# Eight experts of a mixture layer: three passes over split operands on the whole array, or plain float32 on four column strips

## What is computed

```python
logits = xf @ router_w
top_logits, top_idx = lax.top_k(logits, 2)
gates = softmax(top_logits)
# for each expert e, over the tokens that chose it:
y = (silu(xb @ w_gate[e]) * (xb @ w_up[e])) @ w_down[e]      # 1024 -> 3584 -> 1024
out[token] += gate * y
```

## Time and profile before

| | us |
|---|---|
| median of 3 runs | 1414.14 (1412.26 to 1416.24) |
| the profiled execution | 1417.15 |
| its span, first to last instruction | 1415.4 |
| TensorE matmul busy | 1337.0 (94%) |
| TensorE weight load busy | 991.8 |
| DVE busy | 843.4 (60%) |
| ACT busy | 735.3 (52%) |
| granted TensorE clock, mean | 0.98 |
| moved by DMA | 417.39 MB, mean 295 GB/s |

### The profile page before, as it was taken

The page is one execution under the profiler, slowest core; times in us unless marked ns, Lnnn a source line. Parts: engine busy times, 40 slices in busy tenths (PEclk is TensorE's granted clock), DMA queues, the critical chain, the costliest instruction groups (busy, mean ns, idle before and its releaser), DMA issues.

```text
span 1415.4 us, 16234 instructions
## 1 busy us (share of the span) xinstructions
PE 1337.0 (94%) x6696; PEld 991.8 (70%) x6696; DVE 843.4 (60%) x902; ACT 735.3 (52%) x949; POOL 0.2 (0%) x4
## 2 busy tenths in 40 slices
PE   6998999999999799999799999979999999979996
PEld 6776999997786588853378863358888885337885
DVE  4666555555665688820188840078889882009884
ACT  5666444445665477720267730067777772017772
POOL 0000000000000000000000000000000000000000
PEclk9999999999999799999999999989999999999998
DMA  9903553474403089999999999999999999999970
GB/s 361 388 6 119 179 179 120 138 246 171 144 36 119 1 319 362 371 358 407 404 409 408 402 363 409 402 409 409 402 355 347 361 372 358 408 404 409 408 303 31
DMA packets 126688, 417.39 MB, mean 295 GB/s; under 512 B 3344, under 2 KB 8080, under 8 KB 126480
## 3 DMA queue, kind: packets, MB, share of 16 engines
q1 hardware_dynamic: 126608, 416.29, 76.9%
HBM read 415.23 MB, written 1.05 MB: 294 GB/s over the span
## 4 chain that ended last, share of the span: by engine, by line
PE 83%; DMA 6%; DVE 5%; ACT 3%; SPq 2%; issue 1%; DVEq 0%; ACTq 0%
PE ps L506 21%; PE ps L508 21%; PE ps L507 21%; PE ps L925 8%; DMA ring<-moe_g 5%; PE ps L916 2%; SPq L467 2%; PE ps L874 1%; PE ps L488 1%; DVE scratch L1489 1%; DVE ring_lo L1758 1%; DMA ring<-w_in 1%; PE ps L634 1%; ACT scratch L1091 1%; DVE xgT_lo L1764 1%
## 5 line engine op out<-in xcount | busy, mean ns | idle before, releaser
L1758 DVE TENSOR_TENSOR ring_lo<-ring,e_hi 128x2048 fp32r<-128x2048 f32 x210 | 479.3, 2290 | 131.9 <-ACT e_hi L1255 131.6
L1255 ACT ACTIVATE e_hi<-ring 128x2048 fp32r<-128x2048 f32 x210 | 402.4, 1921 | 181.8 <-PE ps L508 156.4
L506 PE MATMUL ps<-e_hi,xgT_hi 128*128 128x512 f32 x560 | 227.9, 407 | 27.9 <-DVE xgT_lo L1764 27.9
L508 PE MATMUL ps<-e_hi,xgT_lo 128*128 128x512 f32 x560 | 223.0, 398 | 0.0
L507 PE MATMUL ps<-ring_lo,xgT_hi 128*128 128x512 f32 x560 | 222.7, 398 | 0.0
L1597 DVE TENSOR_TENSOR d_lo<-ring,d_hi 128x1024 fp32r<-128x1024 f32 x82 | 100.4, 1224 | 95.1 <-ACT d_hi L1199 94.9
L925 PE MATMUL ps<-ring,xgT_s 128*64 128x512 f32 (+1 forms) x768 | 149.5, 542 | 5.2 <-DMA ring<-moe_u 5.2
L506 PEld LDWEIGHTS ps<-e_hi,xgT_hi 128*128 128x128 f32 x560 | 107.1, 191 | 59.0 <-DVE xgT_lo L1764 30.7
L1199 ACT ACTIVATE d_hi<-ring 128x1024 fp32r<-128x1024 f32 x82 | 86.9, 1059 | 112.8 <-PE ps L508 112.8
L508 PEld LDWEIGHTS ps<-e_hi,xgT_lo 128*128 128x128 f32 x560 | 106.9, 191 | 26.4
L507 PEld LDWEIGHTS ps<-ring_lo,xgT_hi 128*128 128x128 f32 x560 | 107.1, 191 | 23.9
(11 more groups left out here) (268 smaller groups left out, 1790.2 us busy)
## 6 DMA issues: line engine op xcount, KB each, us to landing
ring<-moe_g SPq DMA_DIRECT2D x56, 2048.0 KB, 12.9
ring<-moe_u SPq DMA_DIRECT2D x56, 2048.0 KB, 13.8
ring<-moe_d SPq DMA_DIRECT2D x56, 2048.0 KB, 12.5
ring<-w_in SPq DMA_DIRECT2D x6, 2048.0 KB, 11.4
ring<-dense_g SPq DMA_DIRECT2D x5, 2048.0 KB, 7.9
ring<-dense_u SPq DMA_DIRECT2D x5, 2048.0 KB, 7.9
ring<-dense_d SPq DMA_DIRECT2D x5, 2048.0 KB, 8.8
ring<-w_out SPq DMA_DIRECT2D x4, 2048.0 KB, 15.2
```

The source lines that it names most:

```text
L506: pe.matmul(out, hi_l, hi_r, start=start, stop=False, skip_group_check=True)
L508: return pe.matmul(out, lo_l, hi_r, start=False, stop=stop, skip_group_check=True)
L1255: nc.scalar.activation(hi_slot(g, s, q), slot_of(no)[:, r * E_PIECE:(r + 1) * E_PIECE], ACT.Copy).then_inc(act_done, act_p.step((g, s, "le ...
L1758: nc.vector.tensor_tensor(slot_lo(no)[:, part], slot_of(no)[:, part], hi_slot(g, s, q).bitcast(F32), ALU.subtract).then_inc(dve_done, dve_ ...
```

## The change

All eight experts now run as plain float32 with no high and low parts, on four 32-column strips of the array. Tokens are taken in rounds of 32: three rounds for a full expert (room for 96 tokens), two for a small one (64). In a round each of the four strips holds the same 32 tokens and takes a quarter of the weight columns: 256 of 1024, or 128 of the last 512. `e_hi`, `ring_lo`, `xgT_lo`, `hidT_lo`, `y_lo` and their ACT and DVE work are gone; TensorE waits for the unit's DMA alone. The gathered rows' evictions are shared, four chunks on ACT and four on DVE. The gate goes into the scatter matrix (`pick_g`, transposed to `pick_gT`), and the scatter uses four strips of 32 rows, each into a bank of its own. The tables of places are now those of the small expert for all, with one scatter after unit 0. The loop for overflow has two rounds over the experts of 96 tokens each. The last scatter stands behind the `If`, and the output leaves in four quarters, each once it is added, instead of two halves after all.

```diff
-E_PIECE, E_SPLIT = 2048, 4
+STRIP, STRIPS = 32, 4
+BIG, LITTLE = 3, 2
+CAPACITY = [BIG * STRIP] * N_FULL + [LITTLE * STRIP] * (NE - N_FULL)
+ROUNDS = 2
+SCATTER_AFTER = 0
+SCATTER_BANKS = (2, 3, 6, 7)
+HID_T_AFTER = {U_LAST["u", c] + 1: c for c in range(NGU)}
+PICK_T_AFTER = U_LAST["d", 1] + 1
+GATHER_AFTER = U_FIRST["d", NCH - 3]
...
-            sp.wait_ge(result_ready, 1)
-            for a in range(TT):
-                sp.dma_start(out[0, a * P:(a + 1) * P, :], xres[:, a, :]).then_inc(out_stored, 16)
+            for q in range(2 * TT):
+                a, part = q // 2, slice(q % 2 * CH, (q % 2 + 1) * CH)
+                sp.wait_ge(result_ready, q + 1)
+                sp.dma_start(out[0, a * P:(a + 1) * P, part], xres[:, a, part]).then_inc(out_stored, 16)
...
+                def unit(s, it, n):
...
+                    if kind == "d":
+                        for j in range(CH // P):
+                            if c < NCH - 1:
+                                quarter, part, parts = c % 2 * 2 + j // 2, j % 2, 2
+                            else:
+                                quarter, part, parts = j, 0, 1
+                            for t in range(nt):
+                                x0 = (t * parts + part) * P + quarter * STRIP
+                                for q in range(STRIPS):
+                                    ins = pe.matmul(ps[q * STRIP:(q + 1) * STRIP, 4 + t // 2, t % 2 * T:(t % 2 + 1) * T],
+                                                    hidT[:, c // 2 % 2, x0:x0 + STRIP],
+                                                    w[:, j * D + q * T:j * D + (q + 1) * T],
...
+                    else:
+                        cols = GU_COLS[c]
+                        wide, b0 = cols // STRIPS, 0 if kind == "g" else 2
+                        for i in range(UNIT // cols):
+                            k = h * (UNIT // cols) + i
+                            for t in range(nt):
+                                b, c0 = divmod(t * wide, CH)
+                                for q in range(STRIPS):
+                                    ins = pe.matmul(ps[q * STRIP:(q + 1) * STRIP, b0 + b, c0:c0 + wide],
+                                                    xgT[:, k, t * STRIP:(t + 1) * STRIP],
+                                                    w[:, i * cols + q * wide:i * cols + (q + 1) * wide],
...
+                def gates_T(s, it):
+                    pe.wait_ge(act_done, at((g, s, "hidT", 1), it))
+                    for t in range(strips(g, s)):
+                        for a in range(TT):
...
+            def scatter(nt):
+                for t in range(nt):
+                    for a in range(TT):
+                        for q, bank in enumerate(SCATTER_BANKS):
+                            rows_q = slice(q * STRIP, (q + 1) * STRIP)
+                            ins = pe.matmul(ps[:, bank, a * T:(a + 1) * T],
+                                            pick_gT[rows_q, (t * TT + a) * P:(t * TT + a + 1) * P],
+                                            y[rows_q, t * T:(t + 1) * T], ...)
...
-                        nc.scalar.activation(hi_slot(g, s, q), slot_of(no)[:, r * E_PIECE:(r + 1) * E_PIECE],
-                                             ACT.Copy).then_inc(act_done, act_p.step((g, s, "lead", q)))
...
-                        nc.vector.tensor_tensor(slot_lo(no)[:, part], slot_of(no)[:, part], hi_slot(g, s, q).bitcast(F32),
-                                                ALU.subtract).then_inc(dve_done, dve_p.step((g, s, "rest", q)))
```

More of the change, by code:

```diff
@@ L215, in at @@
         if it is None:
-            return start + (NE - 1) * k + m
+            return start + (self.known["trips", loop, name] - 1) * k + m
         assert start + m - back * k > 0
@@ L327, in trunk_program @@
         hT_flat = hT[:, :, :].rearrange("p k t -> p (k t)")
[L328 to L332, removed]
+        sig, hid = hT_flat[:, 0:768], hT_flat[:, 768:1536]
+        rows, y = xn[:, 0, :], xn[:, 1, 0:BIG * T]
+        ps_flat = ps[:, :, :].rearrange("p b n -> p (b n)")
         moved = hT_flat[:, 1024:1024 + 2 * TT * NE * NE].rearrange("p (a e) -> p a e", e=NE)
@@ L773, in gathered_T @@
                             ins.then_inc(pe_done, pe_p.step((g, s, "gathered", k // 4)))
-                def scatter(a, key):
-                    for n in range(2):
-                        part = slice(n * CH, (n + 1) * CH)
-                        pe.matmul(ps[:, 6 + n, :], pickT[:, a * P:(a + 1) * P], y_hi[:, part], start=True, stop=False)
-                        ins = pe.matmul(ps[:, 6 + n, :], pickT[:, a * P:(a + 1) * P], y_lo[:, part], start=False,
-                                        stop=True)
-                        ins.then_inc(pe_done, pe_p.step(key + ("scatter", 2 * a + n)))
@@ new lines, in expert @@
+                def expert(s, it=None):
+                    pe.wait_ge(act_done, at((g, s, "xgT_a")) if g == 0 else before(g, s, it, "xgT_a"))
+                    pe.wait_ge(dve_done, at((g, s, "xgT_d")) if g == 0 else before(g, s, it, "xgT_d"))
+                    for n in range(M_UNITS):
+                        unit(s, it, n)
+                        if n == SCATTER_AFTER and (g or s):
+                            pe.wait_ge(act_done, at((g, s, "y"), it))
+                            scatter(strips_before(g, s)).then_inc(pe_done, pe_p.step((g, s, "scatter")))
+                        if n in HID_T_AFTER:
+                            hidden_T(s, it, HID_T_AFTER[n])
+                        if n == PICK_T_AFTER:
+                            gates_T(s, it)
+                        if n == GATHER_AFTER and (g or s < NE - 1):
+                            pe.wait_ge(act_done, at((g, s, "hidT", 2), it))
@@ L1282, in small_expert @@
[L1282 to L1294 removed]
+                    nt = strips(g, s)
@@ new lines, in expert @@
+                def expert(s, it=None):
+                    if g or s:
+                        dve.wait_ge(pe_done, at((g, s, "scatter"), it))
+                        for q in range(4):
+                            a, n = q // 2, q % 2
+                            part = xres[:, a, n * CH:(n + 1) * CH].rearrange("p (b n) -> p b n", b=2)
+                            b = SCATTER_BANKS[2 * n]
+                            nc.vector.tensor_tensor(part, ps[:, b:b + 2, a * T:(a + 1) * T], part,
+                                                    ALU.add).then_inc(dve_done, dve_p.step((g, s, "add", q)))
+                    for c in range(NGU):
+                        w = strips(g, s) * GU_COLS[c] // STRIPS
+                        dve.wait_ge(act_done, at((g, s, "silu", c), it))
+                        dve.wait_ge(pe_done, at((g, s, "unit", U_LAST["u", c]), it))
+                        nc.vector.tensor_tensor(hid[:, 0:w], ps_flat[:, 2 * CH:2 * CH + w], sig[:, 0:w],
+                                                ALU.mult).then_inc(dve_done, dve_p.step((g, s, "hid", c)))
+                        if c == 2 and (g or s < NE - 1):
+                            dve.wait_ge(pe_done, at((g, s, "pick_g_T"), it))
+                            picks(s if g else s + 1, it + 1 if g else s + 1)
+                    if g or s < NE - 1:
+                        gathered_out(s if g else s + 1, it)
```

514 lines of the change are left out of this document (140 added, 374 removed).

## The result

The changed kernel takes 1391.02 us in the median (1390.13 to 1393.09, 4 runs) against 1413.60 for the kernel before, measured beside it; the ratio is 0.984, 95% interval 0.9821 to 0.9859. That is 22.6 us less where 52 were forecast (1362). The profiled execution took 1391.69 us with a span of 1389.9.

The account below looks back on a forecast made before the run. Full experts were taken as bound by TensorE, small ones by the DMA. Expert times summed to 857 us after 489.7, plus 5 for bookkeeping and 11.5 for the ending, adjusted by +1.8 and -3.0: 1362 us, range 1338 to 1470.

Parts of the forecast that it names:

- PE's blocks of instructions: Expert stage: one 16 KB block in 7 us, 2.4 GB/s of 406; costed at nothing, 6 us as the other end.
- The same 5.17 and 3.45: Two units of the last 512 columns: twice the records at half the length, 5.17 us full and 3.45 small.
- Rival B: Narrow units: a floor per record of 27 to 54 ns; at 54 they double, about 1407 us; chance 0.10.
- Four strips at once, 5.17 and 3.45 for wide units: Wide expert units: four strips run fully concurrently, a unit taking 5.17 us in a full expert, 3.45 in a small one.
- A: Every expert unit: strips cost 8% more than their columns, 1396 us; inside the forecast's range, together chance 0.62.
- C: All expert units: a floor above 54 ns per record makes TensorE's issue the bound, slower than before; chance 0.16.
- D: Expert units: only two strips work at once, units of 10.3 and 6.9 us, about 2096 us; chance 0.09.
- Visits and scatter: Full-array work between units: visits 7.2 us a full expert, 6.3 a small one, scatter 2.9; experts 118.7 and 81.6.
- Returns: Three changes from a small to a full expert: the 7.6 us wait goes, unit 0 starts when it lands.
- The lead: Ring ahead of TensorE: 23.5 us when full, at 5.17 us a unit; small experts take 83.5, 97 and 87 us.
- Start and ending: First unit starts about 487.7, plus 2 us for half speed; after the last unit 11.5 us instead of 14.1.
- E: Overflow loop: lowered capacities overflow, adding 16 more experts, +1900 us; chance 0.03 together with the unforeseen.

Follow-up runs that it names:

- e4: Changed kernel with each matmul of the narrow units split in two of 64 columns, twice the instructions; 1466.06 us (one run).
- e10: Changed kernel with every wide gate and up matmul split in two of 128 columns and each unit's transfer cut to its first quarter; 1377.79 us (one run).
- e1: Changed kernel with each expert unit's weight transfer cut to its first quarter, TensorE's program the same; 1337.86 us (one run).
- e2: Changed kernel with two token rounds of the narrow units on strip pairs with 256 columns, fewer instructions; 1373.29 us, 0.9708 of before.
- e6: Changed kernel with narrow units recut to fewer instructions and four small experts, visited first, fourth, seventh and last; 1360.67 us, 0.9623 of before.

## Why the prediction was wrong, step by step

**The step that failed: PE's blocks of instructions, "I cost it at nothing, with 6 us as the other end".** I had counted right, one block in 7 us, and then weighed the blocks by their bytes: 2.4 GB/s of 406. What counts is the time of a round against the time that TensorE needs for 256 instructions. Under the ring's full traffic the round is 6.2 us (the four blocks from 1132.30 on), with little traffic 3.75 (the idle stretch of e4, and the sum that fitted e10). A wide unit uses 192 instructions in 5.17, a block in 6.9 us: it just fits. A narrow one uses 384, a block in 3.45, and runs dry. Units 16 to 18 of the five full experts took 20.0, 22.3, 22.0, 24.2 and 21.5 us instead of 15.5, 32 us in all. The sum of the full experts shows it: 118.7 forecast, 122.1 to 127.8 measured, 125 to 128 before. Taking it away gave 17.7 (1391.0 to 1373.3); part came back as waiting for landings.

**"The same 5.17 and 3.45" for narrow units.** Rival B named these units and the sign that would show them (7 to 10 us), and gave them 0.10, but with a floor per record as its mechanism. That one falls: 28 ns a record inside the bursts of 128 columns and 14 ns with 64 (e4), and 5.2 us a narrow unit where the traffic is light (e1). The sign "wrong if any TensorE unit of a full expert exceeds 5.9 us" came true in unit 17 of all five and in 16 or 18 of three of them, and so did its reason, that full experts are then no faster than today. By its letter it also caught units with a visit, for which the forecast itself had 6.1 and more.

**Four strips at once, 5.17 and 3.45 for wide units: right.** 5.2 and 3.5 (3.4 with 512 columns), 96 records in 5.06 to 5.2 us. As the forecast said, four records start together (within 21 ns) and the next four 0.216 us after them; in the mean one starts every 53 to 54 ns. Rivals A, C and D fall. The 62 ns per MATMUL that the Trainium skill (TensorE: Matmul & The Clock Gate, "Wait — 56ns, not 53.3ns?") gives for hardware decoding off would put 5.95 us on a wide unit: this trace has 5.2, so it didn't apply here, and no run tells which decoding was on. The floor of about 25 ns between starts that the same section gives doesn't hold across strips either: e4 starts a record every 14 ns on the array, which is one in 56 ns on each strip.

**Visits and scatter: right.** 6.1 for a unit with six transposes (5.17 + 0.92), 7.6 with the gather, 6.3 with the eight transposes, 7.3 and 8.1 with a scatter (8.07 expected). A full expert at 118.4 and a small one at 81.9 in e1, against 118.7 and 81.6.

**ACT and DVE at nothing: right.** Behind the first unit one unit waits for them, 0.6 us (unit 0 of the eighth visit, for an ACT copy), and three quarters of their time is idle. **Returns: right.** Unit 0 of the three full experts behind a small one takes 5.3, 6.7 and 6.1; above 5.2 stand a wait for a landing in the second and mostly that ACT copy in the third.

**The lead: too good by the rate of the transfers.** With 5.17 us a unit I had small experts of 83.5, 97 and 87 us against 81.6 of work, with the returns about 25 us of dry time in all. With the holes gone it is 37 (6.5, 18.1, 9.6 and 2 x 1.5 in e2), and a unit needs 5.27 on the long run (e6). The same bookkeeping with 5.27 gives 102 and 94 for the fourth and the seventh visit, where e2 has 100.0 and 91.6: the rate explains the difference and a little more. By its own numbers the sum was also too kind to the second visit, which gives up 25.0 us of a lead of 23.5. This is the second error: from 1362 to the 1373 of e2 it is 11 us, and from there to 1391 it is the blocks.

**Start and ending.** The first unit began at 483.3 against 487.7. In the other kernels this point lies between 482.9 and 487.0, so these 4.4 us were in part luck, and they hid part of the miss: from the first unit's start to the last unit's end it is 31 us (864 forecast, 895 measured). At half clock the first unit cost 2.8 more where I had 2. The ending took 11.3 against 11.5, by two errors that cancel: 2.3 us before the last scatter in which TensorE waits for nothing shown (a block of instructions lands 1.5 us before their end, and e1 has 2.1 us there with a light DMA; that the branch for the overflow, which stands there, brings them was not tested), and a last store of 2.7 instead of 4.3. **E** didn't happen.

## What to carry to other kernels

When a change makes an engine's instructions shorter, compare the time in which it uses up one block of its program with the spacing of its instruction transfers, and not their bytes with the bandwidth: in these runs 256 instructions had to last 6.2 us beside weights at 400 GB/s, 3.75 beside an idle DMA. A hole after which the clock falls costs more than its own length. Where they don't, use wider operands per instruction (pairs of strips with two token groups instead of four strips with one). And before an engine is made faster, divide the bytes by the rate of a long stretch, not of the best one: that tells how much of the gain the other bound takes back.

## What the runs showed of the hardware that I had not expected

- TensorE's instruction supply depends on other traffic: the same program of 256-instruction blocks took 1595.9 us beside full transfers and 1377.8 beside a quarter of them; block starts were 6.1 us apart in the median in the one, 4.3 in the other.
- A hole of 2.3 us in TensorE's work was followed by 3.4 us at 1.2 GHz (1147.36 to 1150.77), and the first unit after 2.9 us of waiting took 8.0 us; dummy matmuls in that wait kept the clock at 1.00 and the unit at 5.4.
- Records on four strips start every 53 ns with 256 columns, 28 with 128 and 14 with 64, in groups of four within 21 ns: at these rates no strip held up another.
- With 64 columns a group of four starts every 56 ns at a granted clock of 1.00 and every 107 at 0.50 (e4).
